# Modulation tiles out of borrowed buffers and into the plain slabs of a two-layer diffusion backbone

## The reference, cut to what matters

```python
N_MOD = 9; D_MODEL = 1024; D_FF = 2816; DEPTH = 2
silu_c, silu_cc = jax.nn.silu(c), jax.nn.silu(c_ctx)
for i in range(DEPTH):
    mx = jnp.split((silu_c  @ w_mod[i] + b_mod[i])[:, None, :],    N_MOD, axis=-1)
    mc = jnp.split((silu_cc @ w_mod[i] + b_mod[i])[None, None, :], N_MOD, axis=-1)
    x = ffn_sublayer(x, g_norm[i, 0], mx[0], mx[1], mx[2], ffn_w_in[i, 0], ffn_w_out[i, 0])
    h = ffn_sublayer(h, g_norm[i, 0], mc[0], mc[1], mc[2], ffn_w_in[i, 0], ffn_w_out[i, 0])
    ...                                   # mixing uses mx[3..5] and mc[3..5]
    x = ffn_sublayer(x, g_norm[i, 2], mx[6], mx[7], mx[8], ffn_w_in[i, 1], ffn_w_out[i, 1])
    ...                                   # h the same, but not in the last layer
def ffn_sublayer(x, g, shift, scale, gate, w_in, w_out):
    return x + FFN_RES * gate * swiglu(modulate(rms_norm(x, g), shift, scale), w_in, w_out)
```

## Time and profile before

| | us |
|---|---|
| median of 3 runs | 1629.63 (1627.79 to 1630.73) |
| the profiled execution | 1631.09 |
| its span | 1629.3 |
| TensorE busy | 1599.8 (98%) |
| VectorE busy | 1280.1 (79%) |
| ScalarE busy | 671.1 (41%) |
| GpSimd busy | 268.3 (16%) |

### The profile page before, as it was taken

One profiled execution on the slowest core, in us unless ns is written; L12 is line 12 of the kernel. 1 busy time (PEld: TensorE's weight loads), 2 busy tenths in 40 slices (PEclk: granted clock), 3 DMA queues, 4 the chain that ended last, 5 costly groups with the idle time before them and its releaser, 6 DMA issues.

```text
span 1629.3 us, 25834 instructions
## 1 busy us (share of the span) xinstructions
PE 1599.8 (98%) x9846; PEld 1420.7 (87%) x9846; DVE 1280.1 (79%) x2089; ACT 671.1 (41%) x976; POOL 268.3 (16%) x192
## 2 busy tenths in 40 slices
PE   9999999999998999999998999999999999999998
PEld 6788888889877798889988998899899998999997
DVE  5879988888488679888796689888787787666665
ACT  3321222224688532235424342245325456543433
POOL 0000000000598100044124000044033021000000
PEclk8999999999999999999999999999999999999999
DMA  8755655553211236557656346457655332155552
GB/s 329 279 195 207 245 218 201 199 206 108 100 53 53 78 113 237 178 128 180 208 165 171 133 155 245 156 135 182 223 147 150 117 124 72 63 183 193 192 194 78
DMA packets 61423, 268.56 MB, mean 165 GB/s; under 512 B 6944, under 2 KB 7072, under 8 KB 44704
## 3 DMA queue, kind: packets, MB, share of 16 engines
q1 hardware_dynamic: 53280, 252.85, 43.7%
q0 software_dynamic: 8064, 14.68, 5.4%
HBM read 251.78 MB, written 1.05 MB: 155 GB/s over the span
## 4 chain that ended last, share of the span: by engine, by line
PE 82%; DVE 7%; issue 3%; POOL 3%; ACT 2%; DMA 2%; SPq 0%; DVEq 0%; ACTq 0%; POOLq 0%
PE ps L2271 14%; PE ps L2073 10%; PE ps L2074 9%; PE ps L2075 9%; PE ps L2237 7%; PE ps L2238 7%; PE ps L2244 7%; PE ps L2802 5%; PE ps L2100 4%; PE ps L2808 2%; POOL spare L707 2%; PE ps L2421 1%; PE ps L2333 1%; DVE unread L1279 1%; DVE w_lo L1475 1%
## 5 line engine op out<-in xcount | busy, mean ns | idle before, releaser
L2073 PE MATMUL ps<-h_hi,w_lo 128*128 128x512 f32 (+1 forms) x648 | 235.1, 363 | 0.1
L2074 PE MATMUL ps<-h_lo,w_hi 128*128 128x512 f32 (+1 forms) x648 | 233.5, 360 | 0.0
L2075 PE MATMUL ps<-h_hi,w_hi 128*128 128x512 f32 (+1 forms) x648 | 233.4, 360 | 0.0
L2237 PE MATMUL ps<-a_hi,w_hi 128*128 128x512 f32 x512 | 199.5, 390 | 0.9 <-ACT w_hi L946 0.9
L2238 PE MATMUL ps<-a_lo,w_hi 128*128 128x512 f32 x512 | 199.2, 389 | 0.0
L1475 DVE TENSOR_TENSOR w_lo<-raw,w_hi 128x2048 fp32r<-128x2048 f32 x80 | 182.9, 2286 | 16.0 <-ACT w_hi L780 12.2
L780 ACT ACTIVATE w_hi<-raw 128x2048 fp32r<-128x2048 f32 x47 | 90.0, 1914 | 129.1 <-PE ps L2075 123.8
L2073 PEld LDWEIGHTS ps<-h_hi,w_lo 128*128 128x128 f32 x648 | 122.3, 189 | 19.0 <-DVE w_lo L1475 0.7
L2075 PEld LDWEIGHTS ps<-h_hi,w_hi 128*128 128x128 f32 x648 | 122.3, 189 | 18.6
L2074 PEld LDWEIGHTS ps<-h_lo,w_hi 128*128 128x128 f32 x648 | 122.4, 189 | 18.0
L1281 DVE CUSTOM_DVE_ANT_0 mring<-mring,cb 128x1024 f32<-128x1024 f32 x112 | 136.7, 1221 | 0.0
(11 more groups left out here) (409 smaller groups left out, 3796.2 us busy)
## 6 DMA issues: line engine op xcount, KB each, us to landing
raw<-wstream SPq DMA_DIRECT2D x118, 1024.0 KB, 4.9
mring<-wmod SPq DMA_DIRECT2D x128, 512.0 KB, 3.6
extra<-wstream SPq DMA_DIRECT2D x28, 512.0 KB, 4.0
raw<-wstream SPq DMA_DIRECT2D x28, 512.0 KB, 5.3
spare<-wstream SPq DMA_DIRECT2D x11, 1024.0 KB, 4.8
raw<-wstream SPq DMA_DIRECT2D x28, 256.0 KB, 5.4
extra<-extra POOLq DMA_DIRECT2D x28, 256.0 KB, 3.4
raw<-raw POOLq DMA_DIRECT2D x28, 256.0 KB, 4.5
```

The costliest lines, as they stand in the source:

```text
L2073: pe.matmul(dst, lhs_lo, rhs_hi, start=start, stop=False, skip_group_check=True)
L2074: pe.matmul(dst, lhs_hi, rhs_lo, start=False, stop=False, skip_group_check=True)
L2075: return pe.matmul(dst, lhs_hi, rhs_hi, start=False, stop=stop, skip_group_check=True)
L2237: pe.matmul(bank, hi, a_hi[:, k, 0:nt], start=k == 0, stop=False, skip_group_check=True)
```

## The change

The table of tiles is changed: stages 1 and 2 do three tiles in each of the eight slabs of their first group (24, before 20 and 8 borrowed), and none later. The eight tiles that are left over by this go to stage 0: four more in its first group, four more in its second output phase. The borrowed slots (and with them the `slots` argument of `mod_tile`, `mod_dot` and `mod_dots_at`), `late_mods` and VectorE's tiles between the seven-product groups are gone; the four output slabs there are loaded by `plain`, the next group by `fast_loads` from its first slab on. The order of the tiles and their number, 144, stay.

```diff
-MOD_COUNTS = (((2,) * 8, (3,) * 4, (2, 3) * 4, (2,) * 4, (3, 2, 3) * 2), ((2, 3) * 4, (), (), (3, 3, 2, 0), ()),
-              ((2, 3) * 4, (), (), (3, 3, 2, 0), ()), ((),) * 5)
+MOD_COUNTS = (((2, 2, 2, 3, 2, 3, 3, 3), (3,) * 4, (2, 3) * 4, (3,) * 4, (3, 2, 3) * 2),
+              ((3,) * 8, (), (), (), ()), ((3,) * 8, (), (), (), ()), ((),) * 5)
...
-        mod_slots = tuple(mring[:, c] for c in range(4))
-        late_slots = tuple(x.rearrange("p a n -> p (a n)") for x in (sq[:], ss[:], work[:, 0:2], work[:, 2:4]))
...
-            def late_mods(w, f, n):
-                plain(w, w + 3)
-                sp.wait_ge(pair_free, f + 2)
-                for k in range(3):
-                    mod_tile(n + k, (n + k) % 4, n + k - 3, late_slots)
-                sp.wait_ge(hid_ready, f)
-                mod_tile(n + 3, (n + 3) % 4, n, late_slots)
-                plain(w + 3, w + 4)
-                mod_tile(n + 4, (n + 4) % 4, n + 1, late_slots)
-                quarter_loads(w + 4, w % 2, w + 3)
-                for k in range(5, 7):
-                    mod_tile(n + k, (n + k) % 4, n + k - 3, late_slots)
-                quarter_loads(w + 5, (w + 1) % 2, w + 4)
-                mod_tile(n + 7, (n + 7) % 4, n + 4, late_slots)
...
                 fast_loads(w + 12, GROUPS[1])
-                late_mods(w + 20, f, n)
-                n += sum(MOD_COUNTS[s][3])
-                fast_loads(w + 26, GROUPS[2] - 2)
+                plain(w + 20, w + 24)
+                fast_loads(w + 24, GROUPS[2])
...
                         for j in range(2):
-                            out_tiles(sub, b, w, j, nt, None, (0,))
-                            if j == 0 and late[0]:
-                                mod_dots_at(n0, 1, None, late_slots)
-                            out_tiles(sub, b, w, j, nt, None, (1,))
+                            out_tiles(sub, b, w, j, nt)
                             split_lo(w + j + 2, (w + j) % 2)
                             if first:
                                 token_sums(j, T_USE[s])
-                            if late[j]:
-                                done = 1 if j == 0 else 0
-                                mod_dots_at(n0 + done, late[j] - done, None, late_slots)
-                            n0 += late[j]
                         out_tiles(sub, b, w, 2, nt)
                         if first:
                             token_lows(T_USE[s])
                         part_low(0, n, w + 4, 0)
-                        if late[2]:
-                            mod_dots_at(n0, late[2], None, late_slots)
-                        n0 += late[2]
                         part_low(1, n, w + 4, 0)
```

More of the change, by code:

```diff
@@ L565, in slab, with mod_tile @@
                   .then_inc(raw_loaded[slot], 16)
-            def mod_tile(n, slot, wait=None, slots=mod_slots):
+            def mod_tile(n, slot, wait=None):
                 if wait is not None:
                     sp.wait_ge(mod_dots, wait)
-                sp.dma_start(slots[slot], wmod[ds(n, 1)].rearrange("a p n -> p (a n)")) \
+                sp.dma_start(mring[:, slot], wmod[ds(n, 1)].rearrange("a p n -> p (a n)")) \
                   .then_inc(mod_loaded[slot], 16)
@@ L641, in _ @@
             for s in (1, 2):
-                w, f, counts = FFN_W[s], s * FFN_STEPS + GROUPS[0] + GROUPS[1], MOD_COUNTS[s][0]
+                w, counts = FFN_W[s], MOD_COUNTS[s][0]
                 if s == 2:
@@ L1273, in link, with mod_dot @@
                 dve.wait_ge(chain, count[0])
-            def mod_dot(slot, value, n, slots=mod_slots):
+            def mod_dot(slot, value, n):
                 dve.wait_ge(mod_loaded[slot], value)
                 dve.wait_ge(mod_first, n + 1)
-                dve.tensor_tensor_reduce(unread[:], slots[slot], cb[:, 0], 1.0, 0.0,
+                dve.tensor_tensor_reduce(unread[:], mring[:, slot], cb[:, 0], 1.0, 0.0,
                                          ALU.mult, ALU.add, stage[:, 0, slot:slot + 1]).then_inc(mod_first, 1)
-                dve.tensor_tensor_reduce(slots[slot], slots[slot], cb[:, 1], 1.0, 0.0, ALU.mult, ALU.add,
+                dve.tensor_tensor_reduce(mring[:, slot], mring[:, slot], cb[:, 1], 1.0, 0.0, ALU.mult, ALU.add,
                                          stage[:, 1, slot:slot + 1]).then_inc(mod_dots, 1)
@@ L1585, in token_lows, with mod_dots_at @@
                                       ALU.subtract).then_inc(t_low, 1)
-            def mod_dots_at(n, count, i=None, slots=mod_slots):
+            def mod_dots_at(n, count, i=None):
                 for m in range(n, n + count):
-                    mod_dot(m % 4, value_at(i, 8, 16 * (m // 4 + 1)), value_at(i, 2, m), slots)
+                    mod_dot(m % 4, value_at(i, 8, 16 * (m // 4 + 1)), value_at(i, 2, m))
                     if m % 4 == 3:
@@ L1642, in ffn @@
                         first = g + 1 == FAST[s][0]
-                        n, late = FAST_BASE[s, g + 1], list(MOD_COUNTS[s][phase]) or [0] * 4
+                        n = FAST_BASE[s, g + 1]
                         for j in range(2):
-                            out_tiles(sub, b, w, j, nt, None, (0,))
-                            if j == 0 and late[0]:
-                                mod_dots_at(n0, 1, None, late_slots)
-                            out_tiles(sub, b, w, j, nt, None, (1,))
+                            out_tiles(sub, b, w, j, nt)
                             split_lo(w + j + 2, (w + j) % 2)
```

## The result

The changed kernel takes 1622.28 us (median of 6 runs, 1621.76 to 1622.71), the kernel before beside it 1629.68 (6 runs, 1627.79 to 1636.15). The ratio of the two is 0.9950, with a 95% interval of 0.9934 to 0.9965: faster by 7.4 us, or 0.5%. The forecast was 1620.0 us. The profiled execution of the changed kernel took 1622.50 us, its span 1620.7, against 1631.09 and 1629.3 before.

The account below looks back on a forecast made before the run. TensorE was taken as the bound, busy 1599.8 of 1629.3 us. Profiled: 1631.09 - 5.1 - 5.3 + 0.3 = 1621.0; the median less 10.1 is 1619.5; forecast between them 1620.0 us, range 1617.5 to 1627.

Parts of the forecast that it names:

- The stall and its cause: Six-slab groups: late VectorE delays the third slab's load, GpSimd's sums meet the next load; 5.1 and 5.3 us lost.
- The term of 10.4 us: Both six-slab groups behind the borrowed tiles: removing those tiles wins back 5.1 and 5.3 us; bounds 0 to 10.4.
- I charge 0.15 us for it, once in each of the two feed-forwards.: Second output slab's `w_lo` in both later feed-forwards: done at 685.4, wanted at 685.37, nothing left; +0.3 us in all.
- The replay behind it: VectorE's three-tile plain slabs: first product at 605.70, then 2 x 10.28 and 5 x 10.67, last product at 679.6.
- The profiled execution was forecast at 1621.0: Whole kernel, profiled execution: 1631.09 - 5.1 - 5.3 + 0.3 = 1621.0 us.
- Eight tiles more in stage 0: First feed-forward, four tiles in its first group and four in its second output slabs: cost 0.
- The other two close places: Plain group: second slab's `w_hi` with 0.9 us left, last slab's low hidden part with 0.8 left; no charge.
- The lateness passed on to the 8-slab group of stage 2: Third feed-forward: last token low part ends at 1075.5, wanted at 1076.66; 1.1 us left, no wait, bounds 0 to 2.
- the 2 us that I had worked out by that rule: Token low parts ahead of the third feed-forward's 8-slab group: upper bound given as 2 us, no wait in the sum.
- The first (the six-slab group loses without tiles too): Six-slab groups lose the same without the borrowed tiles: 1629.6 us; chance 0.10.
- The second (the loss moves to the 8-slab group): Third feed-forward's 8-slab group takes over the loss, at most one 5.3 us: 1625 us, or 1622; chance 0.12.
- The third (VectorE bounds the plain slabs): Plain slabs in later feed-forwards take 11.7 us against 10.88, some 12 us slower, or more: 1640 us; chance 0.05.

Follow-up runs that it names:

- passes: Changed kernel plus eight spare tiles' passes on VectorE in each of the second and third feed-forward, at the old places, nothing loaded: 1628.45 us, ratio 0.9998.
- transfers without passes: Changed kernel plus the eight tile loads in each of the second and third feed-forward, at their old queue places, no pass over them: 1623.00 us, ratio 0.9962.
- the run with one tile: Changed kernel plus one spare tile's two passes, nothing loaded, behind the last residual ahead of each six-slab group: 1627.82 us, ratio 0.9993.
- seven tiles: Changed kernel plus seven spare tiles' passes in each of the second and third feed-forward, the last of eight left out, nothing loaded: 1622.17 us, ratio 0.9959.
- half a tile: Changed kernel plus one pass (1.15 us of VectorE), nothing loaded, behind the last residual ahead of each six-slab group: 1622.45 us, ratio 0.9952.
- stage 0's tiles alone: Kernel before with the changed kernel's tile counts in the first feed-forward only, borrowed tiles left in the second and third: 1630.43 us, ratio 1.0008.
- Both ways of moving a tile ahead: Changed kernel, second and third feed-forward: first tile done ahead of the first product (1620.68 us; again 1621.47), or plain-slab counts 2, six 3s, 4 (1621.50 us).
- the held load: Kernel before, with the fourth slab's load in each six-slab group waiting until the third slab's two sums have landed: 1635.30 us, ratio 1.0038.
- the version with the early tile: Changed kernel with the first plain slab's first tile done ahead of its product in second and third feed-forward: 1620.68 us, ratio 0.9950; again 1621.47, 0.9947.

## Why the forecast was right, and where it was off

**The stall and its cause: right, and shown but for one link** (from the slow sums to the loss, below the table). Passes without transfers bring it back, transfers without passes do not, and without the load beside them the sums are as quick as ever in stage 1, and nearly so in stage 2, though VectorE is late. Two points of my reading were incomplete. The last tile alone makes the lateness: seven before it fill idle time. And TensorE waits for more than ScalarE's `w_hi`: in the run with one tile it is the row at 876.81 that ends the wait, VectorE's release of PSUM. TensorE's timeline of the kernel before has both waits in stage 1, and in stage 2 the one for `w_hi` is only 0.18 us (at 1222.82):

```profile
866.48 0.39 PE L2271 MATMUL ps<-t_first,w_hi 128*128 128x256 f32 x1 [2.53 <-ACT w_hi L852]
876.02 0.38 PE L2271 MATMUL ps<-a_hi,w_hi 128*128 128x256 f32 x1 [1.74 <-DVE ss L1530]
1233.33 0.39 PE L2271 MATMUL ps<-a_hi,w_hi 128*128 128x256 f32 x1 [2.21 <-DVE ss L1530]
```

What goes with the loss is how far the sums have got when the next load goes out, 13.5 to 13.9 us behind the group's start. The table has the second sum's time, from the view of DMA issues, and when the first of the slab's two sums was launched, behind the group's start:

| profiled group | launched, us | second sum takes, us | loss, us |
|---|---|---|---|
| seven tiles, stage 1 | 9.86 | 4.3 | 0 |
| changed kernel, stage 2 | 9.94 | 5.1 | 0 |
| changed kernel, stage 1 | 11.18 | 6.0 | 0 |
| half a tile, stage 1 | 11.56 | 6.6 | 0 |
| one tile, stage 2 | 11.89 | 6.8 | 0 |
| one tile, stage 1 | 12.32 | 8.5 | 1.88 |
| passes, stage 1 | 12.40 | 8.3 | 1.74 |
| stage 0's tiles alone, stage 2 | 12.58 | 9.0 | 2.64 |
| passes, stage 2 | 12.67 | 9.7 | 5.01 |
| before, stage 2 | 13.30 | 9.4 | 5.44 |
| before, stage 1 | 13.89 | 9.0 | 5.28 |
| stage 0's tiles alone, stage 1 | 13.95 | 9.0 | 5.64 |

In all other profiled groups with the load not held, those of 8 slabs too, the launch came at 9.8 to 11.5 us, the second sum took 4.3 to 6.5, and nothing was lost. So the sums of the changed kernel overlap the next load too in stage 1 and lose nothing: up to 6.8 us in flight are borne, 8.3 are not. That the slow sums, and not the lateness alone, make the loss is read from this table and from the chain of waits; no run kept VectorE late and all sums clear of loads. In the changed kernel the launch came at 9.94 and 11.18 us with the load issued at 3.84 in both: the load itself took 1.2 us longer in stage 1. Why, I did not test.

**The term of 10.4 us.** In the profiled execution it measured 10.7, both groups without loss as forecast (60.39 and 60.40 us, where I took 60.5). But I also took it whole from the median of before. The median fell by 7.4 us and, with the 1.2 that came new, the loss that went was about 8.6 in a middling execution (this is worked out from the medians and read from no trace). The profile before, at 1631.09, was of an execution slower than the median, and its loss was larger. The working says that part of that spread may be the lost time; one end of it still took the full loss off the median (1619.5), and so 1620.0 came out low. Of the 2.3 us by which it did, about 1.8 are this term and 0.9 the step below, less the 0.5 by which I stood above 1619.5.

**The step that failed: "I charge 0.15 us for it, once in each of the two feed-forwards."** The replay behind it was good to 0.05 us: from the first product to the last it gave 73.9 us, and the trace has 680.45 - 606.50 = 73.95. But of the output slabs I asked only the second when its `w_lo` is wanted. The same replay gives the first: product at 679.6 - 10.67 = 668.9, `w_lo` done 5.79 later at 674.7, wanted at 674.49. It was late by 0.2 in my own numbers, and the matmul that waited for it started 0.24 us behind its end (675.55 to 675.79). Measured: 0.50 and 0.11 in stage 1, 0.49 and 0.12 in stage 2, so 1.2 in place of 0.3. The second output slab, where I put the charge, had no wait at all, since the first had moved its due time. Both ways of moving a tile ahead take the 1.2 away in the traces, which shows this cause.

The profiled execution was forecast at 1621.0 and took 1622.5: 0.9 from this step, 0.7 from the longer start, 0.1 from the mixing, less 0.3 in the groups: 1.4 of the 1.5.

**The rest of the parts.** Eight tiles more in stage 0: 0, as forecast, and by a run of its own. The other two close places (the second slab's `w_hi`, the last low hidden part) held. The lateness passed on to the 8-slab group of stage 2: its last token low part ended at 1071.35, 2.05 us ahead of the start where I had 1.1 left, and its load went out 4.62 us behind the start; the group took 80.53 us.

**The rules.** The row `1074.70 3.14 x2` of VectorE's low parts in that group (the same pair takes 2.36 in the kernel before) is stretched by 0.8 us, beside GpSimd's addition at 1074.33; that agrees with the Trainium skill (SBUF — State Buffer, Who interferes with whom), by which the two engines exclude each other. But of the four token low parts none was stretched. Here VectorE kept its pace and GpSimd was held up, an addition of 1.3 us taking 4.37. The profile before already had such a row in this place, an addition of 5.06 us at 1070.14, beside token low parts of 1.22 us each; it would have told me so:

```profile
1069.88 4.37 POOL L736 TENSOR_TENSOR extra<-extra,raw 128x512 f32<-128x512 f32 x1 [1.66 <-DMA extra<-extra]
...
1069.00 1.21 DVE L1565 TENSOR_TENSOR t_second<-sums_second,t_first 128x1024 fp32r<-128x1024 f32 x1
1070.14 1.21 DVE L1565 TENSOR_TENSOR t_third<-sums_third,t_first 128x1024 fp32r<-128x1024 f32 x1
1074.70 3.14 DVE L1465 TENSOR_TENSOR w_lo<-raw,w_hi 128x1024 fp32r<-128x1024 f32 x2
```

So the 2 us that I had worked out by that rule did not come. The other rule (DMA: Bandwidth & Descriptors, Queues, rings and completion order in the Trainium skill), that queues take turns on a DMA engine packet by packet, fits the held load: 4.3 and 5.5 us for the second sum without a load beside it, 8.3 to 9.7 with one that went out about when the sums were launched. Where they met only near the end, the second sum took up to 6.8 us, and TensorE lost nothing.

**The rivals.** The first (the six-slab group loses without tiles too) fell with both groups at 60.4. The second (the loss moves to the 8-slab group) needed sums over 3.5 us later than before; they came at 1088.28 - 1073.40 = 14.9 us, 1.5 later than the 13.4 of the earlier trace rows, and nothing was lost. The third (VectorE bounds the plain slabs) shows only as the 0.2 us by which, in my replay, the row of eight slabs overran, and the 0.5 us ahead of the first output slab that it came to.

## What to carry to other kernels

When a helper engine is late at a point, ask which of its instructions stand behind its last idle time: only those made it late, here one tile of eight, and only those need to move. When a count of how late each thing is has been replayed, ask it for every consumer, the first one above all: the one that waits first moves the due time of those behind it. And where a loss differs between executions, take it from several before it is taken off a median.

## What the runs showed of the hardware that was not expected

GpSimd's queue issued two accumulating DMAs of 256 KB, 0.6 us apart. The first took 3.4 us and the second 4.3 where no load came beside them (3.9 and 5.5 in one group). Where a load from another queue was issued between 0.3 us ahead of the first and 1.3 us behind it, the second took 8.3 to 9.7 us and the first 3.6 to 8.1. Where the load came 1.6 to 3.7 us behind, the second took 4.3 to 6.8. VectorE and GpSimd did not share the delay where their instructions met: here the two token low parts beside it kept their 1.21 us while GpSimd's addition took 4.37; at 839.49 in the kernel before it was VectorE's that took 2.30 in place of 1.22. At the same code the stretch up to the first plain slab took 54.6 to 58.3 us:

```profile
54.62 0.50 PE L2210 MATMUL ps<-a_hi,w_hi 128*128 128x512 f32 x1 [0.46 <-ACT w_hi L927]
```

(the first plain slab in the version with the early tile), and in the run with one tile:

```profile
58.34 0.50 PE L2227 MATMUL ps<-a_hi,w_hi 128*128 128x512 f32 x1 [0.46 <-ACT w_hi L929]
```

What makes it differ was not looked into.
